# Gate and up projections by seven half-size products, weight sums on VectorE, and an earlier start of each feed-forward

## The chip, the core and the metric

One core of a Trainium2 chip runs the whole program. The metric is the time of one execution on the device in microseconds (us); the median of three runs is given. Engines: TensorE (PE; PEld is its weight load), VectorE (DVE), ScalarE (ACT), GpSimd (POOL) and SyncE (SP), which issues most DMAs.

## What is computed

A block of 2 layers over x (256 tokens by 1024, float32), then a second block of 2 layers. Each first-block layer has an attention and convolution mixer and then a feed-forward: dense in layer 0, a mixture of 8 experts in layer 1. Each second-block layer has a feed-forward, a mixer and a feed-forward. The change concerns the five dense feed-forwards:

```python
def swiglu(x, wg, wu, wd):
    return (jax.nn.silu(x @ wg) * (x @ wu)) @ wd
# first block, layer 0: wg, wu 1024 x 3584, wd 3584 x 1024
x = x + swiglu(rms_norm(x, g), wg, wu, wd)
# second block, four times: wg, wu 1024 x 2816, wd 2816 x 1024
mod = silu(c) @ ada_w[l] + ada_b[l]          # shifts, scales and gates
h = h + 0.5 * g1 * swiglu_2(modulate(rms_norm_2(h, g), sh1, sc1), wg, wu, wd)
```

## The kernel before, in words

Every engine has one hand-written program; semaphores join them. The stages are numbered: 0 mix1, 1 ffn1 (F = 3584), 2 mix1, 3 moe, 4 ffn2, 5 mix2, 6 ffn2, 7 ffn2, 8 mix2, 9 ffn2 (F = 2816 in each ffn2). X holds the residual, two blocks of 128 tokens. Between stages each token block is squared and scaled (`squares` and `scale` on ACT, `norm` on DVE), turned by 8 transposes on PE (`turn`), and copied with the norm's gain into XT, 8 chunks of 128 features by 256 tokens.

**A dense feed-forward.** Its unit is a slice f of 128 hidden features; there are F/128 of them, 28 or 22. For each, PE's `ffn` (from line 1829) makes gate and up: 2 times 8 matmuls with 128x128 weights against 256 tokens, into PSUM bank f % 3. One float32 `mm` (line 1769) is two records in the trace. ACT then takes the sigmoid of gate (line 744), and DVE makes two products (lines 1155 and 1157) that leave the slice of the hidden layer in HT. PE is one slice ahead: after the products of slice f it makes the four `down` matmuls of slice f - 1 (512 columns each, accumulated in banks 4 to 7 over the whole stage).

**The weights' ring.** All weights go through `ring`, four slots of 2 MB, filled by SP in one fixed order. A feed-forward's keys alternate: `gu` j (the gate and up columns of slices 2j and 2j+1: two DMAs of 1 MB) and `dn` j (the down rows of the same two slices: one DMA of 1 MB). The load of the key at place i waits until the key at place i - 4 is given back, so `gu` j + 2 takes the slot of `gu` j, and `dn` j + 1 that of `dn` j - 1. SP's program (line 495) is strictly in order: `dn` j + 1, then `gu` j + 2, then `dn` j + 2:

```python
rg.plan(("gu", st, j), s_gu(st, 2 * j + 2), parts=2)
rg.plan(("dn", st, j), s_dn(st, j + 1) if 2 * j < nf - 4 else s_y(st, 4))
```

`s_gu(st, 2j + 2)` comes when PE has made the gate and up of slice 2j + 1; `s_dn(st, j + 1)` when it has made `down` of slice 2j + 1.

**The conditioning.** `mod` needs 36 pieces of ada_w (2 MB each), loaded by ACT's queue (`ada_load`, line 733), multiplied and summed by DVE (`ada_sum`, lines 1129 and 1132, eight instructions), and turned into MODC (`ada`, `ada_out`) four pieces at a time. These lie in stages 1 (20 pieces), 4 (8) and 6 (8).

**The end.** The last `down` matmuls of each 128 tokens by 512 columns are given to DVE (`s_y`), which adds them to X. For ffn2 this is `residual`, lines 1180 and 1182. `gate_rows` makes the gates' row (16 records on PE, line 1769, `C,MODC`).

Of the kernel before, what the change touches and what calls it, by code (L numbers as in the profile page):

```python
# [15 lines left out]
P = 128  # L16
# [7 lines left out]
F2 = 2816  # L24
# [105 lines left out]
def build(nc, A, out):  # L130
    with ExitStack() as ctx:
# [25 lines left out]
        EG = QT[:, 0:2, :]  # L157
# [65 lines left out]

        ADA_W = ((GS[:, :, :],), (R[:, 2048:4608].rearrange("p (c n) -> p c n", c=5),
# [15 lines left out]
        FG = M2[:, 2048:3072]  # L240
# [46 lines left out]
        s_xta = signal("s_xta", mix1=4, ffn1=4, moe=4, ffn2=4, mix2=4)  # L287
# [5 lines left out]
        s_gu = signal("s_gu", ffn1=28, ffn2=22)  # L293
        s_sig = signal("s_sig", ffn1=28, moe=16, ffn2=22)
        s_silu = signal("s_silu", ffn1=28, moe=16, ffn2=22)
        s_h = signal("s_h", ffn1=28, moe=16, ffn2=22)
# [117 lines left out]
        ADA_SUM, ADA_MM, ADA_OUT = {}, {}, {}  # L414
        for st, first, batches, unit in ((1, 0, 5, lambda b, i: 5 * b + i + 1), (4, 20, 2, lambda b, i: 9 * b + 2 * i + 1),
                                         (6, 28, 2, lambda b, i: 9 * b + 2 * i + 1)):
            for b in range(batches):
                for i in range(4):
                    ADA_SUM[st, unit(b, i)] = first + 4 * b + i
                ADA_MM[st, unit(b, 3) + 1] = first // 4 + b  # L420
                ADA_OUT[st, unit(b, 3) + 2] = first // 4 + b
        ADA_FIRST = {1: 0, 4: 20, 6: 28}
        ADA_LAST = {1: 20, 4: 28, 6: 36}
# [50 lines left out]
        PT1 = np.cumsum([0] + NKC1).tolist()  # L474

# [188 lines left out]
        def _(e):  # L664
# [28 lines left out]
            def squares(st):  # L693

                for b in range(2):
# [3 lines left out]
                    scale(st + 1, b)  # L699

            def turn(st, gain, shift=None):
                base = 4 if st in (1, 3) else 0
# [14 lines left out]
            def gate_rows(st):  # L717

                for h in range(2):
                    e.wait_ge(*s_gbt(st, h + 1))  # L720
                    e.activation(GB[:, h * 512:h * 512 + 512], PS[:, 4 + h, :], ACT.Copy,
# [14 lines left out]
            def ffn(st, F):  # L736
                if st in ADA_LAST:
                    ada_load(ADA_FIRST[st])
                    ada_load(ADA_FIRST[st] + 1)
                for f in range(F // P):  # L740
                    e.wait_ge(*s_gu(st, f + 1))
                    if f >= 2:
                        e.wait_ge(*s_h(st, f - 1))
                    e.activation(EG[:, f % 2, :], PS[:, f % 3, 0:256], ACT.Sigmoid).then_inc(s_sig.sem, 1)  # L744
                    if (st, f) in ADA_SUM and ADA_SUM[st, f] + 2 < ADA_LAST[st]:
                        ada_load(ADA_SUM[st, f] + 2)
                squares(st)
# [128 lines left out]
            def moe(st):  # L876
# [12 lines left out]
                def turned(n):  # L889
# [12 lines left out]
                for n, (ex, f, W) in enumerate(ROUNDS):  # L902
                    if n:
                        turned(n - 1)
# [12 lines left out]
                turned(15)  # L917
# [9 lines left out]
                for b in range(2):  # L927
                    scale(st + 1, b)
# [22 lines left out]
            def mix2(st, l):  # L951
                turn_mod(st, l, 1)
                gate_rows(st)
# [90 lines left out]
            turn(1, lambda c: vcol("ffn_norm_g", 0, c))  # L1044
# [3 lines left out]
            for l in range(2):  # L1048
                st = 4 + 3 * l
                turn_mod(st, l, 0)  # L1050
                gate_rows(st)
                ffn(st, F2)
                mix2(st + 1, l)
                turn_mod(st + 2, l, 2)
                gate_rows(st + 2)
# [4 lines left out]
        def _(e):  # L1060
# [40 lines left out]
            def turn(st, gain, shift=None):  # L1101
                base = 4 if st in (1, 3) else 0
# [1383 lines left out]
```

## Time and profile before

| | us |
|---|---|
| runs shown | 3113.36, 3119.49, 3120.49; median 3119.49 |
| the profiled execution, its own time | 3116.34 |
| its span (first to last instruction) | 3114.5 |
| PE busy | 2968.5 (95% of the span) |
| DVE busy | 823.8 (26%) |
| ACT busy | 395.1 (13%) |
| mean granted TensorE clock | 0.975 |

A row of the profile has line, engine, operation, tiles and shapes, the count, the busy time in us and the mean duration of one in ns. Matmuls are pipelined and the ends that the trace gives them are modelled, so the pace of a stream is read from the starts of two neighbouring groups, not from the mean duration.

### The profile page before, as it was taken

The numbers are of one execution on the slowest core, as the hardware profiler recorded it, in microseconds if no ns is written. First come the engines' busy times: TensorE is split into PE (matmuls) and PEld (weight loads), VectorE is DVE, ScalarE is ACT, GpSimd is POOL, SyncE is SP. The second block draws the span as 40 slices with busy tenths as digits, with TensorE's granted clock in tenths as the row PEclk, the third lists the DMA queues.
The fourth block names the chain that finished last, engine by engine and source line by source line (L and its number), as shares of the span: only waits on it lengthen the run. The fifth ranks groups of instructions, "written<-read, shape, count | busy, mean of one in ns | idle before, by whom it ended". The sixth has DMA issues, their size and how long they took to land.

```text
span 3114.5 us, 34448 instructions
## 1 busy us (share of the span) xinstructions
PE 2968.5 (95%) x15102; PEld 1777.4 (57%) x15102; DVE 823.8 (26%) x1717; ACT 395.1 (13%) x1015; POOL 153.4 (5%) x221
## 2 busy tenths in 40 slices
PE   7699999889999999999997999999999999999998
PEld 5457776543333333333334776586776776576776
DVE  4735453741000000000001333242333002242002
ACT  4420003430000000000001001131001001131000
POOL 6200003300000000000000000000000000000000
PEclk9899999889999999999998999999999999999999
DMA  6149884317999999999996764324764444413442
GB/s 218 68 150 318 286 304 152 116 55 268 377 371 393 358 368 393 358 368 391 359 372 231 260 213 162 122 90 154 257 216 136 149 152 154 140 55 135 149 142 94
DMA packets 266289, 704.58 MB, mean 226 GB/s; under 512 B 9286, under 2 KB 132439, under 8 KB 241556
## 3 DMA queue, kind: packets, MB, share of 16 engines
q1 hardware_dynamic: 225072, 622.39, 54.7%
q10 hardware_dynamic: 38036, 75.61, 6.9%
q0 software_dynamic: 3024, 4.31, 0.5%
q8 instruction: 121, 1.98, 0.3%
q14 instruction: 36, 0.29, 0.0%
HBM read 698.07 MB, written 1.05 MB: 224 GB/s over the span
## 4 chain that ended last, share of the span: by engine, by line
PE 87%; DVE 7%; DMA 3%; ACT 2%; issue 1%; POOL 0%; DVEq 0%; SPq 0%; ACTq 0%
PE PS L1769 84%; DMA ring<-in_moe_w_up_dram 2%; DVE PS L1271 1%; DMA ring<-in_w_in_dram 1%; PE PS L2151 1%; PE PS L1986 0%; DVE SM L1398 0%; DVE SM L1652 0%; DVE GS L1324 0%; ACT R L1004 0%; PE PS L1795 0%; ACT R L685 0%; PE PS L2359 0%; DVE PS L1649 0%; DVE R L1246 0%
## 5 line engine op out<-in xcount | busy, mean ns | idle before, releaser
L1769 PE MATMUL PS<-XT,ring 128*128 128x256 f32 x4480 | 1003.9, 383 | 11.8 <-ACT GS L984 8.0
L1769 PEld LDWEIGHTS PS<-XT,ring 128*128 128x128 f32 x4480 | 857.4, 192 | 178.8 <-issue 56.3
L1769 PE MATMUL PS<-ring,R 128*32 128x256 f32 (+2 forms) x3616 | 718.6, 489 | 0.6 <-ACT R L893 0.6
L1769 PEld LDWEIGHTS PS<-ring,R 128*32 128x32 f32 (+2 forms) x3616 | 291.2, 137 | 367.3 <-issue 330.7
L1769 PE MATMUL PS<-ring,GS 128*64 128x384 f32 (+4 forms) x2176 | 305.2, 527 | 1.0 <-ACT XT L913 0.8
L1769 PE MATMUL PS<-ring,KZ 128*64 128x512 f32 (+3 forms) x2048 | 301.8, 543 | 0.6 <-DMA ring<-in_moe_w_up_dram 0.5
L1155 DVE TENSOR_TENSOR QT<-QT,PS 128x256 f32<-128x256 f32 x116 | 48.9, 421 | 828.3 <-ACT QT L744 828.3
L1769 PEld LDWEIGHTS PS<-ring,GS 128*32 128x32 f32 (+1 forms) x2176 | 103.3, 122 | 197.5 <-issue 192.8
L1769 PEld LDWEIGHTS PS<-ring,KZ 128*64 128x64 f32 (+1 forms) x2048 | 99.7, 123 | 196.8 <-issue 190.8
L1769 PE MATMUL PS<-ring,XT 128*128 128x512 f32 (+2 forms) x512 | 197.9, 548 | 1.2 <-ACT XT L708 1.2
L744 ACT ACTIVATE QT<-PS 128x256 f32<-128x256 f32 x116 | 44.5, 384 | 1092.7 <-PE PS L1769 1092.7
L1769 PEld LDWEIGHTS PS<-ring,XT 128*128 128x128 f32 x512 | 98.1, 192 | 98.9 <-issue 93.7
L1542 DVE TENSOR_TENSOR QT<-QT,PS 128x1536 f32<-128x1536 f32 (+1 forms) x16 | 24.9, 1554 | 439.4 <-PE PS L1769 439.4
L893 ACT ACTIVATE R<-PS 128x512 f32<-128x512 f32 (+1 forms) x32 | 17.4, 544 | 638.2 <-PE PS L2151 638.2
L1132 DVE SCALAR_TENSOR_TENSOR KZ<-GS,CACT,KZ 128x512 f32<-128x512 f32 x126 | 94.7, 752 | 4.5
L1132 DVE SCALAR_TENSOR_TENSOR KZ<-R,CACT,KZ 128x512 f32<-128x512 f32 x126 | 94.7, 752 | 4.5
L626 POOL TENSOR_TENSOR M<-M,GS 128x256 f32<-128x256 f32 x120 | 87.5, 748 | 49.7 <-ACT GS L773 45.5
L1530 DVE TENSOR_TENSOR QT<-QT,PS 128x1536 f32<-128x1536 f32 (+1 forms) x16 | 24.9, 1554 | 179.5 <-ACT QT L908 179.5
L1769 PE MATMUL PS<-ring,MT 128*128 128x512 f32 x128 | 62.4, 638 | 0.0
L650 POOL DMA_DIRECT2D R<-R x16 | 8.4, 527 | 1019.2 <-ACT R L899 1019.2
L1769 PE MATMUL PS<-KZ,QT 128*128 128x256 f32 (+1 forms) x256 | 55.4, 362 | 2.8 <-ACT R L843 2.4
L1769 PE MATMUL PS<-ring,QT 128*128 128x512 f32 x128 | 55.5, 594 | 2.5 <-DVE QT L1739 2.5
(320 smaller groups left out, 1660.3 us busy)
## 6 DMA issues: line engine op xcount, KB each, us to landing
ring<-in_moe_w_gate_dram SPq DMA_DIRECT2D x32, 2048.0 KB, 11.1
ring<-in_moe_w_up_dram SPq DMA_DIRECT2D x32, 2048.0 KB, 10.9
ring<-in_moe_w_down_dram SPq DMA_DIRECT2D x32, 2048.0 KB, 10.9
ring<-in_moe_w_gate_dram SPq DMA_DIRECT2D x32, 1536.0 KB, 11.3
ring<-in_moe_w_up_dram SPq DMA_DIRECT2D x32, 1536.0 KB, 7.1
ring<-in_moe_w_down_dram SPq DMA_DIRECT2D x32, 1536.0 KB, 8.4
ring<-in_ffn_wg_dram SPq DMA_DIRECT2D x44, 1024.0 KB, 5.5
ring<-in_ffn_wu_dram SPq DMA_DIRECT2D x44, 1024.0 KB, 8.0
```

What stands on the lines that cost most here:

```text
L626: e.tensor_tensor(Y[:, ch, :], Y[:, ch, :], CTP[:, m % 8, :], ADD).then_inc(s_cadd.sem, 1)
L650: e.dma_start(YS[0:64, 512 * h:512 * h + 512], YC[64 * h:64 * h + 64, 0:512]).then_inc(s_ys.sem, 16)
L744: e.activation(EG[:, f % 2, :], PS[:, f % 3, 0:256], ACT.Sigmoid).then_inc(s_sig.sem, 1)
L893: e.activation(HM[:, r, 0:W], PS[:, 3 + r, 0:W], ACT.Copy).then_inc(s_hta.sem, 1)
L1132: w = e.scalar_tensor_tensor(out=acc, in0=rows[c], scalar=CACT[:, 1, c:c + 1], in1=acc, op0=MUL, op1=ADD)
L1155: e.tensor_tensor(ev, ev, PS[:, f % 3, 0:256], MUL).then_inc(s_silu.sem, 1)
L1271: t = e.scalar_tensor_tensor(out=y, in0=h, scalar=w, in1=y, op0=MUL, op1=ADD)
L1530: e.tensor_tensor(h, h, PS[:, 0:3, 0:W], MUL).then_inc(s_silu.sem, 1)
L1542: e.tensor_tensor(h, h, PS[:, 3:6, 0:W], MUL).then_inc(s_h.sem, 1)
L1769: return e.matmul(o, lhsT, rhs, start=first, stop=last)
L2151: w = e.transpose(PS[:, 3 + r, c * P:c * P + P], h[:, c, :], ident)
```

## The change

Pairs of slices take the place of slices: the unit is now j, with 256 hidden features, and there are 14 of them in stage 1 and 11 in each ffn2. The multiplication of 256 tokens by 1024 features by 256 hidden features is split into halves in all three directions. For gate and up each, seven products of halves take the place of eight (Winograd's form of Strassen's method). Product m of pair j is 2 times 4 `mm`s with 128x128 weights against 128 tokens, 16 records. Three of the seven use the weights as loaded. The other four use sums of weight blocks, `t_sum(st, j, 1)` to `(st, j, 4)`, each one DVE instruction of 1024 elements per partition; the third overwrites a block of `gu` j in the ring. The token side has four sums (SS) per stage, 512 elements each. ACT copies product 1 out of PSUM (CP). DVE joins the products in seven additions of 256 elements (`join`); the sigmoid and the two products behind it work on 512 elements.

On PE the order in a pair is product 1, 2, 6, 5, 7, 3, 4 and then all eight `down` matmuls of pair j - 1. Product 4 goes to the place of product 1 in PSUM and waits for the join `u2`. `gu` j is given back when product 4 of pair j is made; `dn` j as before. SP's own code is not touched.

At a stage's beginning, products 1 and 2 of pair 0 and product 1 of pair 1, which need the first token block only, stand before the second block's transposes (`turn_block`); the first block's transposes stand inside the stage before, and three weight sums (`ahead`) before DVE's last additions of that stage. `gate_rows` comes after product 2 of pair 1. The 36 pieces of the conditioning lie in stages 1 (12), 4 (8), 6 (8) and 7 (8), one per pair.

The core of the diff:

```diff
+        TS = [[x.rearrange("p (u c n) -> p u c n", u=2, c=4) for x in y]
+              for y in ((M2[:, 1024:2048], M2[:, 2048:3072], QTF[:, 0:1024]),
+                        (MTF[:, 0:1024], MTF[:, 1024:2048], OA[:, :, :].rearrange("p b n -> p (b n)")))]
+        SS = [R[:, i:i + 512].rearrange("p (c n) -> p c n", c=4) for i in (7168, 7680, 4608, 5120)]
+        U2, U3, U4 = (QTF[:, i:i + 256].rearrange("p (u n) -> p u n", u=2) for i in (1024, 1280, 1536))
+        CP = [x.rearrange("p (u n) -> p u n", u=2) for x in (QTF[:, 1792:2048], R[:, 8192:8448])]
...
+        FIRST2 = [(0, 1), (0, 2), (1, 1), (1, 2)]
+        PRODUCTS = FIRST2 + [(j, m) for j in range(14) for m in (1, 2, 6, 5, 7, 3, 4) if (j, m) not in FIRST2]
+        SUMS = ("c11", "u2", "u4", "u3", "c12", "c22", "c21")
...
-        ADA_FIRST = {1: 0, 4: 20, 6: 28}
-        ADA_LAST = {1: 20, 4: 28, 6: 36}
+                ADA_OUT[st, 4 * b + 5] = first // 4 + b
+        ADA_FIRST = {1: 0, 4: 12, 6: 20, 7: 28}
+        ADA_LAST = {1: 12, 4: 20, 6: 28, 7: 36}
...
-                rg.plan(("gu", st, j), s_gu(st, 2 * j + 2), parts=2)
+                rg.plan(("gu", st, j), made(st, j, 4), parts=2)
...
+        def product_bank(j, m):
+
+            if m in (1, 2, 4):
+                return 3 if j == 1 else 0, 256 * (m == 2)
+            return (1, 256 * (m == 5)) if m in (6, 5) else (2, 256 * (m == 3))
+
...
+                def copy(j):
+
+                    e.wait_ge(*made(st, j, 2))
+                    if j >= 2:
+                        e.wait_ge(*joined(st, j - 2, "u2"))
+                    e.activation(CP[j % 2], product_of(j, 1), ACT.Copy).then_inc(s_cp.sem, 1)
+
+                copy(0)
+                turned(st, 1, (0, 1, 4, 5))
+                copy(1)
+                if st > 1:
+                    gate_rows(st, 6)
                 if st in ADA_LAST:
                     ada_load(ADA_FIRST[st])
                     ada_load(ADA_FIRST[st] + 1)
...
+            def t_sum(st, j, n):
+
+                w = rg.view(("gu", st, j), 16, 256).rearrange("p (u c) n -> p u c n", u=2)
+                b11, b12, b21, b22 = (w[:, :, 4 * k:4 * k + 4, P * m:P * m + P] for k in range(2) for m in range(2))
+                t1, t2, t4 = TS[j % 2]
+                if n == 1:
+                    e.wait_ge(*rg.landed["gu", st, j])
+                    if j >= 2:
+                        e.wait_ge(*made(st, j - 2, 4))
+                    e.tensor_tensor(t1, b12, b11, SUB).then_inc(s_ts.sem, 1)
+                elif n == 2:
+                    e.wait_ge(*s_ts(st, 4 * j + 1))
+                    e.tensor_tensor(t2, b22, t1, SUB).then_inc(s_ts.sem, 1)
+                elif n == 3:
+                    e.tensor_tensor(b12, b22, b12, SUB).then_inc(s_ts.sem, 1)
+                else:
+                    e.wait_ge(*s_ts(st, 4 * j + 2))
+                    e.tensor_tensor(t4, b21, t2, SUB).then_inc(s_ts.sem, 1)
+
...
+                for n in (1, 2, 3):
+                    t_sum(st, 0, n)
...
-                for f in range(F // P):
-                    ev = EG[:, f % 2, :]
-                    e.wait_ge(*s_sig(st, f + 1))
-                    e.tensor_tensor(ev, ev, PS[:, f % 3, 0:256], MUL).then_inc(s_silu.sem, 1)
-                    e.wait_ge(*s_silu(st, f + 1))
-                    e.tensor_tensor(HT[:, f % 8, :], ev, PS[:, f % 3, 256:512], MUL).then_inc(s_h.sem, 1)
-                    if (st, f) in ADA_OUT:
...
+                e.tensor_tensor(SS[0], a21, a22, ADD).then_inc(s_ss.sem, 1)
+                e.wait_ge(*s_ss(st, 1))
+                e.tensor_tensor(SS[1], SS[0], a11, SUB).then_inc(s_ss.sem, 1)
+                e.tensor_tensor(SS[2], a11, a21, SUB).then_inc(s_ss.sem, 1)
+                e.wait_ge(*s_ss(st, 2))
+                e.tensor_tensor(SS[3], a12, SS[1], SUB).then_inc(s_ss.sem, 1)
+                t_sum(st, 0, 4)
+                n = F // 256
+                for j in range(n):
+                    if j + 1 < n:
+                        for m in range(1, 5):
+                            t_sum(st, j + 1, m)
+                    def join(r, out, x, y):
+                        e.tensor_tensor(out, x, y, ADD).then_inc(s_cq.sem, 1)
+
+                    e.wait_ge(*s_cp(st, j + 1))
+                    if j:
+                        e.wait_ge(*s_h(st, j))
+                    join("c11", CQ[:, :, 0, :], CP[j % 2], product_of(j, 2))
+                    e.wait_ge(*made(st, j, 5))
+                    join("u2", U2, CP[j % 2], product_of(j, 6))
+                    e.wait_ge(*joined(st, j, "u2"))
+                    join("u4", U4, U2, product_of(j, 5))
+                    e.wait_ge(*made(st, j, 3))
+                    join("u3", U3, U2, product_of(j, 7))
+                    e.wait_ge(*joined(st, j, "u4"))
+                    join("c12", CQ[:, :, 2, :], U4, product_of(j, 3))
+                    e.wait_ge(*joined(st, j, "u3"))
+                    join("c22", CQ[:, :, 3, :], U3, product_of(j, 5))
+                    e.wait_ge(*made(st, j, 4))
+                    join("c21", CQ[:, :, 1, :], U3, product_of(j, 4))
+                    gq, uq = (CQ[:, u, :, :].rearrange("p q n -> p (q n)") for u in range(2))
+                    e.wait_ge(*s_sig(st, j + 1))
+                    e.tensor_tensor(SIG, SIG, gq, MUL).then_inc(s_silu.sem, 1)
+                    e.wait_ge(*s_silu(st, j + 1))
+                    at = 2 * j % 8
+                    e.tensor_tensor(HT[:, at:at + 2, :].rearrange("p c n -> p (c n)"), SIG, uq, MUL).then_inc(s_h.sem, 1)
...
+                def product(j, m):
+                    key = ("gu", st, j)
+                    w = rg.view(key, 16, 256).rearrange("p (u c) n -> p u c n", u=2)
+                    b11, t3, b21, b22 = (w[:, :, 4 * k:4 * k + 4, P * i:P * i + P] for k in range(2) for i in range(2))
+                    t1, t2, t4 = TS[j % 2]
+                    a11, a12, a22 = XT[:, 0:4, 0:P], XT[:, 4:8, 0:P], XT[:, 4:8, P:2 * P]
+                    wt, x = {1: (b11, a11), 2: (b21, a12), 3: (b22, SS[3]), 4: (t4, a22), 5: (t1, SS[0]), 6: (t2, SS[1]),
+                             7: (t3, SS[2])}[m]
+                    B, at = product_bank(j, m)
+                    if m == 1:
+                        e.wait_ge(*rg.landed[key])
+                        if j == 1 and st == 1:
+                            e.wait_ge(*s_x(0, 4))
+                        elif j > 1:
+                            e.wait_ge(*joined(st, j - 1 if j > 2 else 0, "c21"))
+                    elif m == 6:
+                        if j == 0:
+                            e.wait_ge(*s_ss(st, 2))
+                        else:
+                            e.wait_ge(*joined(st, j - 1, "c22"))
+                        e.wait_ge(*s_ts(st, 4 * j + 2))
+                    elif m == 7:
+                        if j == 0:
+                            e.wait_ge(*s_ss(st, 3))
+                        e.wait_ge(*s_ts(st, 4 * j + 3))
+                    elif m == 3:
+                        if j == 0:
+                            e.wait_ge(*s_ss(st, 4))
+                    elif m == 4:
+                        e.wait_ge(*joined(st, j, "u2"))
+                        e.wait_ge(*s_ts(st, 4 * j + 4))
+                    for u in range(2):
+                        for c in range(4):
+                            if j == 0 and u == 0 and m in (1, 2):
+                                e.wait_ge(*s_xta(st, 4 * (m - 1) + c + 1))
+                            w = mm(PS[:, B, at + u * P:at + u * P + P], wt[:, u, c, :], x[:, c, :], c == 0, c == 3)
+                    w.then_inc(s_m.sem, 1)
 
                 def down(f, b, h):
...
+                product(0, 1)
+                product(0, 2)
+                product(1, 1)
+                turn_block(st, 1)
+                product(1, 2)
+                if st > 1:
+                    l, k = mod_of(st)
+                    gate_rows(st, l, 3 * k + 2, 6)()
+                for j in range(n):
+                    for m in (1, 2, 6, 5, 7, 3, 4):
+                        if j > 1 or m not in (1, 2):
+                            product(j, m)
+                    d = j - 1
+                    if 0 <= d < n - 2:
+                        if d == 0:
+                            if st > 1:
+                                e.wait_ge(*s_gbm(st, 2))
+                        e.wait_ge(*rg.landed["dn", st, d])
                         e.wait_ge(*s_h(st, d + 1))
-                        for b in range(2):
-                            for h in range(2):
-                                w = down(d, b, h)
-                        if d % 2:
-                            w.then_inc(s_dn.sem, 1)
-                    if (st, f) in ADA_MM:
-                        ada(ADA_MM[st, f])
-                for b in range(2):
+                        for f in (2 * d, 2 * d + 1):
+                            for b in range(2):
+                                for h in range(2):
...
+                        if b == 1 and h == 0:
+                            turn_block(st + 1, 0)
```

Order on DVE, one pair of stage 1. Before (L1155 and L1157 are the two products of a slice, L1129 and L1132 a piece of the conditioning):

```order
L1155 TENSOR_TENSOR QT<-QT,PS 128x256 [waits s_sig]
L1157 TENSOR_TENSOR R<-QT,PS 128x256 [waits s_silu]
L1129 TENSOR_SCALAR KZ<-R,CACT 128x512 [waits s_ada1]
L1132 SCALAR_TENSOR_TENSOR KZ<-R,CACT,KZ 128x512 [waits s_vector] x7
L1155 TENSOR_TENSOR QT<-QT,PS 128x256 [waits s_sig]
L1157 TENSOR_TENSOR R<-QT,PS 128x256 [waits s_silu]
```

Now (L1213 to L1221 are the four weight sums of pair j + 1, L1291 the joins of pair j, the second of them u2; s_ring0 is the landing of `gu` j + 1, s_m counts products made):

```order
L1213 TENSOR_TENSOR M<-ring 128x1024 [waits s_m,s_ring0]
L1216 TENSOR_TENSOR M<-ring,M 128x1024 [waits s_ts]
L1218 TENSOR_TENSOR ring<-ring 128x2x4x128
L1221 TENSOR_TENSOR QT<-ring,M 128x1024 [waits s_ts]
L1291 TENSOR_TENSOR M<-R,PS 128x2x128 [waits s_h,s_cp]
L1291 TENSOR_TENSOR QT<-R,PS 128x256 [waits s_m]
L1291 TENSOR_TENSOR QT<-QT,PS 128x256 [waits s_cq]
L1291 TENSOR_TENSOR QT<-QT,PS 128x256 [waits s_m]
L1291 TENSOR_TENSOR M<-QT,PS 128x2x128 [waits s_cq] x2
L1291 TENSOR_TENSOR M<-QT,PS 128x2x128 [waits s_m]
L1311 TENSOR_TENSOR KZ<-KZ,M 128x512 [waits s_sig]
L1314 TENSOR_TENSOR R<-KZ,M 128x512 [waits s_silu]
```

The sums of the next pair, with their wait for the ring, stand ahead of all joins of this pair.

Order on PE, one pair of stage 1. Before (128x256 is gate and up of a slice, 128x512 the down products of the slice before):

```order
L1769 MATMUL PS<-XT,ring 128x256 [waits s_h,s_ring2]
L1769 MATMUL PS<-XT,ring 128x256 x15
L1769 MATMUL PS<-ring,R 128x512 [waits s_h]
L1769 MATMUL PS<-ring,R 128x512 x3
L1769 MATMUL PS<-XT,ring 128x256 [waits s_h]
L1769 MATMUL PS<-XT,ring 128x256 x15
L1769 MATMUL PS<-ring,R 128x512 [waits s_h,s_ring3]
L1769 MATMUL PS<-ring,R 128x512 x3
```

Now (products 1 and 2; 6 and 5; 7 and 3; 4; then the down products of pair j - 1; s_cq counts joins, s_ts weight sums):

```order
L1930 MATMUL PS<-XT,ring 128x128 [waits s_cq,s_ring2]
L1930 MATMUL PS<-XT,ring 128x128 x15
L1930 MATMUL PS<-R,MT 128x128 [waits s_ts,s_cq]
L1930 MATMUL PS<-R,MT 128x128 x15
L1930 MATMUL PS<-R,ring 128x128 [waits s_ts]
L1930 MATMUL PS<-R,ring 128x128 x15
L1930 MATMUL PS<-XT,OA 128x128 [waits s_ts,s_cq]
L1930 MATMUL PS<-XT,OA 128x128 x7
L1930 MATMUL PS<-ring,R 128x512 [waits s_h,s_ring1]
L1930 MATMUL PS<-ring,R 128x512 x7
```

Down products, which before stood behind each slice, now stand together behind product 4, and product 4 has a wait for a join.

## Rows read from the trace of the kernel before

**Rows 1.** The page's first part and chain, whole kernel.

```profile
PE 2968.5 (95%) x15102; PEld 1777.4 (57%) x15102; DVE 823.8 (26%) x1717; ACT 395.1 (13%) x1015; POOL 153.4 (5%) x221
...
PE 87%; DVE 7%; DMA 3%; ACT 2%; issue 1%; POOL 0%; DVEq 0%; SPq 0%; ACTq 0%
```

**Rows 2.** Timeline of PE, stage 7: start us, us, engine, line, operation, tiles, count.

```profile
2474.48 7.07 PE L1769 MATMUL PS<-XT,ring 128*128 128x256 f32 x32
2481.39 3.60 PE L1769 MATMUL PS<-ring,R 128*128 128x512 f32 x8
2484.82 7.07 PE L1769 MATMUL PS<-XT,ring 128*128 128x256 f32 x32
...
2495.16 2.10 PE L1769 MATMUL PS<-XT,ring 128*128 128x256 f32 x9
```

**Rows 3.** Timeline of SP's DMA issues, same stretch.

```profile
2474.68 0.37 SPq L495 DMA_DIRECT2D ring<-in_ffn_wd_dram  x1
2481.58 0.37 SPq L495 DMA_DIRECT2D ring<-in_ffn_wg_dram  x1
2481.99 0.58 SPq L495 DMA_DIRECT2D ring<-in_ffn_wu_dram  x1
2495.36 0.37 SPq L495 DMA_DIRECT2D ring<-in_ffn_wd_dram  x1
```

**Rows 4.** Timeline of PE: streams of 128 columns and what follows them, clock 1.00.

```profile
2048.94 1.06 PE L1769 MATMUL PS<-R 128*128 128x128 f32 x8
2049.83 3.62 PE L1769 MATMUL PS<-XT,ring 128*128 128x256 f32 x16
...
2092.61 1.04 PE L2359 MATMUL PS<-C,R 128*128 128x128 f32 x8
2093.49 1.90 PE L1769 MATMUL PS<-R 128*128 128x64 f32 x16
```

**Rows 5.** Groups by line and form, PE's weight loads with 256 columns, whole kernel.

```profile
L1769 PEld LDWEIGHTS PS<-XT,ring 128*128 128x128 f32 x4480 | 857.4, 192 | 178.8 <-issue 56.3 <-ACT GS L984 8.0 <-DMA ring<-in_w_in_dram 1.7
```

**Rows 6.** Groups by line and form, DVE, whole kernel: busy us, mean ns.

```profile
L1132 DVE SCALAR_TENSOR_TENSOR KZ<-GS,CACT,KZ 128x512 f32<-128x512 f32 x126 | 94.7, 752 | 4.5
...
L1155 DVE TENSOR_TENSOR QT<-QT,PS 128x256 f32<-128x256 f32 x116 | 48.9, 421 | 828.3 <-ACT QT L744 828.3
...
L1182 DVE TENSOR_TENSOR X<-X,M 128x512 f32<-128x512 f32 x24 | 16.6, 692 | 0.8
...
L1711 DVE TENSOR_TENSOR M<-M,SM 128x1024 f32<-128x1024 f32 x2 | 2.4, 1224 | 0.1
```

**Rows 7.** DMA issues at 2482 and 2495, then at 302 beside conditioning: KB, us to landing.

```profile
ring<-in_ffn_wg_dram SPq DMA_DIRECT2D x1, 1024.0 KB, 5.4
ring<-in_ffn_wu_dram SPq DMA_DIRECT2D x1, 1024.0 KB, 7.9
...
ring<-in_ffn_wd_dram SPq DMA_DIRECT2D x1, 1024.0 KB, 5.0
...
ring<-in_ffn_w_gate_dram SPq DMA_DIRECT2D x1, 1024.0 KB, 9.3
ring<-in_ffn_w_up_dram SPq DMA_DIRECT2D x1, 1024.0 KB, 12.4
```

**Rows 8.** Windows: PE, PEld, DVE, ACT, POOL busy us (x), PEclk, DMA share, GB/s.

```profile
2162.00:2164.00 2.00, 0.00 (x0) 0.00 (x0) 1.67 (x8) 0.68 (x1) 0.00 (x0) 1.00 0.77 315
...
2166.00:2168.00 2.00, 2.00 (x5) 1.61 (x6) 0.76 (x2) 1.98 (x5) 0.00 (x0) 0.50 0.75 172
2168.00:2169.00 1.00, 1.00 (x5) 0.86 (x4) 0.00 (x0) 0.84 (x1) 0.00 (x0) 0.85 1.04 403
...
2083.00:2089.00 6.00, 6.00 (x26) 5.55 (x25) 0.42 (x1) 0.61 (x2) 0.00 (x0) 0.50 0.00 0
...
2485.00:2489.00 4.00, 4.00 (x20) 3.51 (x20) 0.00 (x0) 0.00 (x0) 0.00 (x0) 1.00 1.09 353
```

**Rows 9.** The chain in time, from stage 6 to stage 7.

```profile
2384.69 12.46 PE PS L1769 x29
...
2402.07 0.45 PE PS L1795 x2
...
2403.77 46.33 PE PS L1769 x182
```

More of the change, by code:

```diff
@@ L739, in ffn @@
                     ada_load(ADA_FIRST[st] + 1)
-                for f in range(F // P):
[L741 to L746, printed above, removed]
+                for j in range(F // 256):
+                    if j >= 2:
+                        copy(j)
+                    k = ADA_SUM.get((st, j - 1))
+                    if k is not None and k + 2 < ADA_LAST[st]:
+                        ada_load(k + 2)
+                    e.wait_ge(*joined(st, j, "c21"))
+                    if j:
+                        e.wait_ge(*s_h(st, j))
+                    e.activation(SIG, CQ[:, 0, :, :].rearrange("p q n -> p (q n)"), ACT.Sigmoid).then_inc(s_sig.sem, 1)
                 squares(st)
@@ L1162, in ffn @@
+                if STAGES[(st + 1) % 10] == "ffn2":
+                    ahead(st + 1)
                 for b in range(2):
@@ L1870, in ffn @@
-                for b in range(2):
-                    for h in range(2):
-                        for f in range(nf - 4, nf):
-                            if b == h == 0:
-                                if f % 2 == 0:
-                                    e.wait_ge(*rg.landed["dn", st, f // 2])
-                                e.wait_ge(*s_h(st, f + 1))
-                            w = down(f, b, h)
-                        w.then_inc(s_y.sem, 1)
+                              f == 0, f == last)
@@ new lines, in ffn @@
+                e.wait_ge(*rg.landed["dn", st, n - 2])
+                e.wait_ge(*s_h(st, n - 1))
+                for f in (last - 3, last - 2):
+                    for h in range(2):
+                        down(f, 0, h)
+                e.wait_ge(*rg.landed["dn", st, n - 1])
+                e.wait_ge(*s_h(st, n))
+                for h in range(2):
+                    down(last - 1, 0, h)
+                    down(last, 0, h).then_inc(s_y.sem, 1)
+                for h in range(2):
+                    for f in range(last - 3, last + 1):
+                        if h == 1 and f == last - 1 and STAGES[(st + 1) % 10] == "ffn2":
+                            turn_block(st + 1, 0)
+                        w = down(f, 1, h)
+                    w.then_inc(s_y.sem, 1)
@@ L2063, in mix1 @@
                     for h in range(2):
-                        out(b, h, range(4))
+                        if st == 0 and b == h == 1:
+                            out(b, h, range(2))
+                            turn_block(1, 0)
+                            out(b, h, range(2, 4))
+                        else:
+                            out(b, h, range(4))
             def moe(st):
```

192 lines of the change are left out of this document (119 added, 73 removed).

## The prediction

> **What bounds the kernel now.** I read the page first: PE is busy for 95% of the span and holds 87% of the chain [rows 1]. So a microsecond taken off PE inside a stage counts in full, and one added to PE's wait counts too. Then I read PE's timeline in a feed-forward without conditioning work [rows 2]. From the start of 32 records of 256 columns to the start of the next group are 2481.39 - 2474.48 = 6.91 us, 216 ns each. Eight records of 512 columns take 2484.82 - 2481.39 = 3.43 us, 429 ns each. A slice is 10.34 us, a pair of slices 20.68, and there is no gap. SP's issues [rows 3] show why the ring costs nothing now: down's 1 MB goes out at 2474.68, gate and up only 6.9 us later, and nobody needs them for most of a pair.
>
> **The products.** A pair now has 7 x 16 = 112 records of 128 columns for 64 of 256. Streams of 128 columns exist already [rows 4]: 8 records take 2049.83 - 2048.94 = 0.89 us, and 2093.49 - 2092.61 = 0.88 us, so 110 to 112 ns each. The risk is the weight load: a record of the old kind carries a load of 192 ns on average [rows 5], which hid behind 216 ns of matmul. But 192 cannot be its least duration, since 8 loads passed in 0.89 us. Bounds are 110 and 192 ns; I take 111, the rate of the rows of just this shape. A product is then 16 x 0.111 = 1.78 us, seven are 12.43 against 64 x 0.216 = 13.82. That saves 1.39 us per pair, and 14 + 4 x 11 = 58 pairs save 81 us, if nothing waits. The down products stay: 16 x 0.429 = 6.86 us.
>
> The Trainium skill (TensorE: Matmul & The Clock Gate, "Back-to-back issue gap") says that pairs of load and matmul of 128 columns keep up about 81 ns where the columns alone would give 56, and this speaks against the change. An estimate by that ratio, 108 x 81/56 = 156 ns, would make seven products 17.5 us, 3.7 more than before. The rows above, of eight records, do not agree with it; no longer stream of this shape stands in the trace.
>
> **DVE's work per pair.** Four weight sums of 1024 elements at 1.224 us [rows 6] are 4.9 us, 5.0 with the gaps between them. Seven joins at about 0.42 and two products of 512 at 0.69 make 4.3 us. A piece of conditioning is 7 x 0.752 plus about 0.48, 5.7 us. Together 15.0 us of a pair of 19: by busy time DVE fits. What counts is the order.
>
> **The new wait, and what stands behind it.** Follow one pair j from the moment S at which PE starts product 1.
> 1. SP issues in order. `dn` j waits for the down products of pair j - 2, and on PE these are the last thing before S. `gu` j + 1 stands behind `dn` j on SP. Its own slot has been free since product 4 of pair j - 1, 6.86 us earlier; before the change that was the later event, now it is the earlier one. So three DMAs of 1 MB go out together at S.
> 2. When does `up` land? Issued as a pair, gate lands after 5.4 and up 7.9 us after its own issue; down alone takes 5.0 [rows 7]. With issue times of 0.4 us each [rows 3] up lands at S + 0.9 + 7.9 = 8.8, if the third megabyte in front costs nothing. At the 353 GB/s of a full stretch [rows 8] 1 MB is 3.0 us, somewhat less for down's longer rows: 11.4. I take 11.0, near the upper end, since the same DMA engines are full in that stretch. Beside a conditioning load of 2 MB, up took 12.4 instead of 7.9 [rows 7], 4.5 more. I take 3.5 more, 14.5, because that load is issued some 4 us after S; bounds 11 and 16.
> 3. DVE's four sums of pair j + 1 wait for this landing and stand ahead of all joins of pair j. `u2` is ready 5.0 + two joins of 0.42 + 0.06, together 5.9 us later: at S + 16.9, or at S + 20.4 with conditioning.
> 4. PE reaches product 4 at S + 6 x 1.78 = 10.7 and waits for `u2`: 6.2 us, or 9.7.
> 5. Then product 4 (1.78) and the down products (6.86), and the next S. Nothing shortens this chain: each link starts from S.
>
> DVE itself is free in time: after product 4 one join, sigmoid, two products and a piece of conditioning take about 2.5 + 5.7 = 8.2 us, which is 1.4 us after the next S, long before the landing.
>
> **The clock.** While PE stands for 2 us the granted clock is still 1.00; after the gap of which that is a part it is 0.50 (1.2 instead of 2.4 GHz) until 2168.15 or so, and in another place for over 6 us [rows 8]. A wait of 6 us will bring it down each time. Work that takes 3 to 6.4 us at half clock loses 1.5 to 3.2 us; I take 2.4 for each stall. The stall then costs 6.2 + 2.4 = 8.6 us, with conditioning 12.1.
>
> **How often.** Pair 0 has its next weights in the ring, the last pair has no next one. Pair 1: its products 1 and 2 are made early, and `gu` 2 goes out alone after product 4 of pair 0, landing 0.5 + 7.9 = 8.4 later; u2 at 14.3 against four products, 7.1: 7.2 + 2.4 = 9.6 us. So 5 x 9.6 = 48; of the 43 others 10 + 3 x 6 = 28 lie beside a conditioning load, 28 x 12.1 = 339, and 15 x 8.6 = 129. Sum 516 us.
>
> **The stage boundaries.** Now 2403.77 - 2397.15 = 6.6 us pass from the last down product to the first product of the next stage, and second-block transposes start at 2402.07 [rows 9]. The same chain of additions, squares, norm and scaling stays for the second token block, but three products, 5.3 us, move into it. Against that gate_rows (16 records, 1.8 us) comes onto PE's path in ffn2, the 1.2 us of copying before the first product is covered, and pair 0 waits 0.8 us for u2 behind DVE's longer list (copies, four token sums, five weight sums). Net -3.9 us for each ffn2 and -5.7 for stage 1, together -21. DVE's three sums ahead of the last additions, 3.7 us, delay the first block's norm; PE has 9 us of down products there, which hide it, and if that cover is gone up to 3 us per boundary come back. The pieces of conditioning are as many as before and hide under PE both times; only their loads matter, counted above.
>
> **Sum.** -81 - 21 + 516 = +414 on the 3116.3 us of the profiled execution: 3530 us. The median of the runs is 3 us above that execution, which I leave inside the range.
>
> **Rivals.**
> *The ring is in time and the change gains.* This ends on the other side. Its mechanism is `u2` at or before S + 10.7, so up landed by S + 4.8. Then only -102 remain: 3014 us. For it: the slot of `gu` j + 1 is free 6.9 us before S, so an issue then would land in time; DVE has room. Against: the order of SP's list, unchanged in the diff, and 1 MB alone takes 5.0 us. It decides where stalls average 102/48 = 2.1 us, that is up landing about 6.9 us after S; above that the kernel is slower. I give it 0.12, for a misread order rather than for fast DMAs.
>
> *The weight loads set the pace.* If each record of 128 columns takes its load's mean of 192 ns, a product is 3.07 us and a pair 7 x 3.07 + 6.86 = 28.4 us, +7.7; 58 pairs give +446, and beside conditioning u2 (20.4) still comes 2 us after six products (18.4), +56, boundaries -20: about 3600 us. For it stands the mean load duration, against it the rows of 110 to 112 ns. 0.05. The ratio of the Trainium skill above (TensorE: Matmul & The Clock Gate) would go the same way; the trace's short streams do not agree with it.
>
> *Gain and stalls cancel*, because up lands around 7 us after S: 3116 us, 0.02.
>
> *The forecast*, stalls in 48 pairs: 0.81.
>
> **Numbers.** The likeliest case gives 3530. Its low end takes 8.8 and 11 us to landing and 1.5 for the clock: 5.5 and 7.7 us per stall, 8.7 for pair 1, -102 + 44 + 83 + 216 = +241, 3357. Its high end takes 11.4 and 16 and 3.2: 9.8, 14.4 and 10.4, -102 + 52 + 147 + 403 = +500, 3616. I widen the low end a little, since links that I added up may overlap: 3330 to 3620. The gaining case lies outside and holds 0.12. A measurement of this kernel tells about 0.3% from no change: faster 0.12, same 0.02, slower 0.86.
>
> **What would show it.** Right: PE idle before product 4 (`XT,QT` and `XT,OA` of 128 columns) of 5 to 10 us in nearly every pair, released by DVE's join; the first weight sum (1024 elements, out of the ring) waiting for the DMA of up; down, gate and up issued within 1 us of each other; a pair of 26 to 32 us; the clock at 0.50 behind each wait. Products 1 to 3 and 5 to 7 at 110 to 112 ns a record. Wrong: pairs of 19 us with PE dense, or products paced at 150 ns and more with no wait before product 4.

## The result, and the profile after

| | before | after |
|---|---|---|
| median of four runs, us | 3118.97 (3113.36 to 3120.49) | 3576.44 (3573.73 to 3584.68) |
| profiled execution, span | 3116.34, 3114.5 | 3573.73, 3571.2 |
| PE busy | 95% | 84% |
| mean granted clock | 0.975 | 0.912 |

The changed kernel takes 1.147 times as long (95% interval 1.145 to 1.150): slower by 457 us, where the prediction had 414.

Page of the changed kernel, the first part and the chain:

```profile
PE 3000.8 (84%) x17886; PEld 1888.7 (53%) x17886; DVE 1236.5 (35%) x2259; ACT 420.6 (12%) x1055; POOL 152.6 (4%) x221
...
PE 63%; DMA 19%; DVE 13%; issue 2%; ACT 1%; SPq 1%; DVEq 0%; POOL 0%; ACTq 0%
```

Against [rows 1] the chain has lost PE and gained DMA and DVE, together 32% for 10%: the last work to end now waits for transfers and for the sums on them. That PE is busy for slightly longer than before (3000.8 against 2968.5 us), with an eighth less work in gate and up, is the clock; more on it below.

PE's waits of the changed kernel (engine, tile and line, releaser: us in total, times, longest), the row of the stall and the one of gate and up's own load:

```profile
PE PS L1930 <- DVE QT L1291: 429.4, 49, 12.6
...
PE PS L1930 <- DMA ring<-in_ffn_wu_dram: 7.5, 1, 7.5
```

One pair of stage 9, without conditioning: PE's timeline, then SP's issues.

```profile
3344.03 3.73 PE L1930 MATMUL PS<-XT,ring 128*128 128x128 f32 x32
3347.60 3.74 PE L1930 MATMUL PS<-R,MT 128*128 128x128 f32 x32
3351.17 3.74 PE L1930 MATMUL PS<-R,ring 128*128 128x128 f32 x32
3360.67 3.71 PE L1930 MATMUL PS<-XT,OA 128*128 128x128 f32 x16 [5.76 <-DVE QT L1291]
3364.22 7.03 PE L1930 MATMUL PS<-ring,R 128*128 128x512 f32 x16
3371.08 1.17 PE L1930 MATMUL PS<-XT,ring 128*128 128x128 f32 x9
```

```profile
3344.22 0.37 SPq L549 DMA_DIRECT2D ring<-in_ffn_wd_dram  x1
3344.64 0.47 SPq L549 DMA_DIRECT2D ring<-in_ffn_wg_dram  x1
3345.15 0.58 SPq L549 DMA_DIRECT2D ring<-in_ffn_wu_dram  x1
3371.28 0.37 SPq L549 DMA_DIRECT2D ring<-in_ffn_wd_dram  x1
```

Six products pass without a gap, 3.57 us for two, so 111.6 ns a record. Then PE stands for 5.76 us before product 4. A pair takes 27.05 us, where it took 20.68 [rows 2]. SP issues three loads within a microsecond of each other at the pair's start; before, gate and up's issue stood 6.9 us behind down's [rows 3] and the ring was never late. The same pair in the chain of waits, in time (start us, us, what):

```profile
3344.22 0.37 SPq L549
...
3345.15 10.03 DMA ring<-in_ffn_wu_dram
...
3355.20 1.24 DVE M L1213
...
3356.46 1.23 DVE M L1216
...
3358.74 1.22 DVE QT L1221
...
3360.29 0.34 DVE QT L1291
...
3360.67 10.59 PE PS L1930 x32
```

Every link of the loop is here: down's issue (released by PE's last down product), the transfer of up, four sums, two joins, product 4 with the down products, and the next issue. PE's first six products, 10.7 us, are not in it; transfer, sums and joins take 16.4 us beside them. Beside conditioning (stage 1) it is the transfer that is longer, 16.73 us:

```profile
278.72 0.37 SPq L549
...
279.64 16.73 DMA ring<-in_ffn_w_up_dram
...
296.40 1.24 DVE M L1213
...
301.87 10.81 PE PS L1930 x32
```

I went through all 43 pairs that are neither a stage's first two nor its last. From down's issue, up lands after 10.8 to 11.0 us in 14 of them, after 12 to 13 in 6, and after 15.2 to 17.8 in 23. From landing to product 4 it is 5.5 us in every one. The longest of these pairs takes 34.2 us.

### The profile page after: what moved, and what is told of

Same layout as the page of the kernel before. It is cut to its first block, busy times and chain, and to the rows that moved or that the text cites. A ratio compares the mean times of both kernels' runs of the same rounds, so it can differ in the third digit from the quotient of the medians.

```text
span 3571.2 us, 40818 instructions
## 1 busy us (share of the span) xinstructions
PE 3000.8 (84%) x17886; PEld 1888.7 (53%) x17886; DVE 1236.5 (35%) x2259; ACT 420.6 (12%) x1055; POOL 152.6 (4%) x221
## 4 chain that ended last, share of the span: by engine, by line
PE 63%; DMA 19%; DVE 13%; issue 2%; ACT 1%; SPq 1%; DVEq 0%; POOL 0%; ACTq 0%
PE PS L1930 61%; DMA ring<-in_ffn_wu_dram 13%; DMA ring<-in_ffn_w_up_dram 5%; DVE PS L1428 1%; SPq L549 1%; DVE M L1213 1%; DVE QT L1221 1%; DVE M L1216 1%; DVE MT L1213 1%; DVE MT L1216 1%; DVE OA L1221 1%; DMA ring<-in_w_in_dram 1%; PE PS L2367 1%; DVE QT L1291 0%; DVE M L1291 0%
## 5 line engine op out<-in xcount | busy, mean ns | idle before, releaser
L1930 PE MATMUL PS<-XT,ring 128*128 128x128 f32 (+1 forms) x2624 | 400.0, 311 | 16.1 <-ACT GS L1070 7.9
L1930 PEld LDWEIGHTS PS<-XT,ring 128*128 128x128 f32 x2624 | 367.5, 195 | 68.0 <-issue 30.4
L1930 PE MATMUL PS<-XT,OA 128*128 128x128 f32 x432 | 99.6, 424 | 248.3 <-DVE QT L1291 248.3
L1930 PE MATMUL PS<-XT,QT 128*128 128x128 f32 x496 | 99.5, 382 | 181.1 <-DVE QT L1291 181.1
L1930 PEld LDWEIGHTS PS<-XT,OA 128*128 128x128 f32 x432 | 92.2, 324 | 253.2 <-DVE QT L1291 253.2
L1930 PE MATMUL PS<-R,ring 128*128 128x128 f32 x1856 | 216.7, 275 | 0.0
L1930 PEld LDWEIGHTS PS<-R,ring 128*128 128x128 f32 x1856 | 211.9, 192 | 0.0
L1930 PEld LDWEIGHTS PS<-XT,QT 128*128 128x128 f32 x496 | 92.4, 287 | 185.9 <-DVE QT L1291 185.4
L1213 DVE TENSOR_TENSOR M<-ring 128x1024 f32<-128x1024 f32 x31 | 38.0, 1225 | 372.2 <-DMA ring<-in_ffn_wu_dram 276.2
L1291 DVE TENSOR_TENSOR M<-QT,PS 128x256 f32<-128x256 f32 x205 | 80.6, 416 | 139.1 <-PE PS L1930 121.0
L1213 DVE TENSOR_TENSOR MT<-ring 128x1024 f32<-128x1024 f32 x27 | 33.1, 1224 | 265.1 <-DMA ring<-in_ffn_wu_dram 198.2
L1930 PE MATMUL PS<-R,M 128*128 128x128 f32 (+1 forms) x1024 | 121.1, 279 | 1.0 <-DVE R L1280 1.0
```

The lines of the kernel that those rows point to most:

```text
L1213: e.tensor_tensor(t1, b12, b11, SUB).then_inc(s_ts.sem, 1)
L1291: e.tensor_tensor(out, x, y, ADD).then_inc(s_cq.sem, 1)
L1930: return e.matmul(o, lhsT, rhs, start=first, stop=last)
```

## The experiments

The kernel before ran beside these on the same chip: 3119.88 us for `e1` to `e4`, 3118.65 for `e5` to `e8`.

**The order of the loads alone.** `e1_gu_first` lets gate and up of the next pair go ahead of this pair's down, in the ring's plan and in SP's list (the plan's part is shown):

```diff
-            for j in range(nf // 2):
-                rg.plan(("gu", st, j), made(st, j, 4), parts=2)
-                rg.plan(("dn", st, j), s_dn(st, j + 1) if 2 * j < nf - 4 else s_y(st, 4))
+            n = nf // 2
+            rg.plan(("gu", st, 0), made(st, 0, 4), parts=2)
+            for j in range(n):
+                if j + 1 < n:
+                    rg.plan(("gu", st, j + 1), made(st, j + 1, 4), parts=2)
+                rg.plan(("dn", st, j), s_dn(st, j + 1) if j < n - 2 else s_y(st, 4))
```

> One edit to the changed kernel: in the ring's order gate and up of pair j + 1 stand ahead of down of pair j, so that their load is issued when product 4 of pair j - 1 is made, 6.9 us before S, and not behind the down products. Theory (SP's order makes the wait): up lands 1.5 us after S, about 6 us beside a conditioning load; u2 is ready before PE reaches product 4 in plain pairs and 1 us late beside conditioning. A plain pair takes 19.3 us, one with conditioning 20 to 21; the whole 3020 to 3060 us, below the kernel before. Rival (the DMA engines are simply too slow for the weights and the conditioning): the waits stay for the most part, over 3400 us. Rival (weight loads set the pace of 128 columns): the waits go, but a product takes 2.5 to 3.1 us and the whole stays over 3250.

Measured: 3032.94 us (3029.50 to 3034.78), 0.972 of before (0.971 to 0.974). SP's issues and PE's timeline, stage 7:

```profile
2395.47 0.37 SPq L552 DMA_DIRECT2D ring<-in_ffn_wg_dram  x1
2395.88 0.58 SPq L552 DMA_DIRECT2D ring<-in_ffn_wu_dram  x1
2402.34 0.37 SPq L552 DMA_DIRECT2D ring<-in_ffn_wd_dram  x1
```

```profile
2382.77 3.73 PE L1939 MATMUL PS<-XT,ring 128*128 128x128 f32 x32
...
2393.49 1.95 PE L1939 MATMUL PS<-XT,QT 128*128 128x128 f32 x16
2395.27 7.03 PE L1939 MATMUL PS<-ring,R 128*128 128x512 f32 x16
2402.14 3.73 PE L1939 MATMUL PS<-XT,ring 128*128 128x128 f32 x32
```

Gate and up go out as PE leaves product 4, 6.9 us before the pair ends, and a pair is 2402.14 - 2382.77 = 19.37 us without a gap. The same transfers, sums and products as in the changed kernel, in another order on one queue, are worth 543 us. Of PE's wait for the joins this is left:

```profile
PE PS L1939 <- DVE QT L1300: 11.2, 11, 1.4
```

**The order of the sums alone.** `e2_sums_late` keeps SP's order and moves DVE's four sums of pair j + 1 behind the joins of pair j and the two DVE products that make its slice of HT (in `ffn` of DVE, for the same `j + 1 < n`):

```diff
-                    if j + 1 < n:
-                        for m in range(1, 5):
-                            t_sum(st, j + 1, m)
                     def join(r, out, x, y):
...
                     e.tensor_tensor(HT[:, at:at + 2, :].rearrange("p c n -> p (c n)"), SIG, uq, MUL).then_inc(s_h.sem, 1)
+                    if j + 1 < n:
+                        for m in range(1, 5):
+                            t_sum(st, j + 1, m)
```

> One edit to the changed kernel: DVE makes the four weight sums of pair j + 1 behind the last product of pair j and no longer ahead of its joins; SP's order stays. Theory (it is DVE's order that passes the late landing on to product 4): up still lands 11 and 17 us after S, but nobody waits for it; the joins run beside the products, PE does not wait before product 4, and the sums are ready some 3 us before product 6 of the next pair. 3020 to 3060 us. Rival (PE is held by the landing itself, by another way): waits of PE move to product 1 or 6 of the next pair, over 3300 us.

Measured: 3067.87 us (3066.84 to 3068.98), 0.984 of before (0.982 to 0.985). The load still goes out late, and costs hardly anything: `u2` no longer stands behind it. So the stall needs both links, the late issue and the sums ahead of the joins; cutting either frees PE. What is left is one new wait, and one that the changed kernel had too (stage 7, below):

```profile
PE PS L1930 <- DVE MT L1216: 25.6, 5, 5.1
...
PE PS L1930 <- DMA ring<-in_ffn_wu_dram: 7.4, 1, 7.4
```

**Both.** `e3_both` has both edits.

> Both edits together. If each takes the whole wait away, they do not add: within 0.5% of the better of the two, 3010 to 3040 us, pairs of 19.3 us throughout. If each leaves a part, the sum is lower than either by that part. The forecast without waits was 3014 us.

Measured: 3055.82 us (3051.12 to 3056.29), 0.979 (0.978 to 0.981). That is 23 us slower than the first edit alone, a miss. The place is the start of each stage: PE's timeline, then DVE's, stage 1.

```profile
220.25 5.97 PE L1939 MATMUL PS<-R,MT 128*128 128x128 f32 x32 [5.11 <-DVE MT L1225]
226.06 3.74 PE L1939 MATMUL PS<-R,ring 128*128 128x128 f32 x32
```

```profile
217.02 0.69 DVE L1320 TENSOR_TENSOR R<-KZ,M 128x512 f32<-128x512 f32 x1
217.63 1.22 DVE L1222 TENSOR_TENSOR MT<-ring 128x1024 f32<-128x1024 f32 x1
218.88 1.23 DVE L1225 TENSOR_TENSOR MT<-ring,MT 128x1024 f32<-128x1024 f32 x1
```

Pair 1 has two products made early and no down products before it, so its product 6 comes right behind product 4 of pair 0. Its sums stood last in DVE's row, behind all joins of pair 0. The wait is 5.1 us, five times, and the 32 records behind it take 226.06 - 220.25 = 5.81 instead of 3.57 us (5.0 to 6.4 in the five stages). The waits of 25.6 us and the 11 us of slower records are 37; the 11 us of waits that `e1_gu_first` still had are gone, and 26 remain for the 23 measured.

**That miss mended.** `e5_pair1_early` is `e3_both` with the sums of pair 1 ahead of the joins of pair 0, those of the later pairs behind:

```diff
+                    if j == 0:
+                        for m in range(1, 5):
+                            t_sum(st, 1, m)
                     def join(r, out, x, y):
...
-                    if j + 1 < n:
+                    if 0 < j < n - 1:
                         for m in range(1, 5):
                             t_sum(st, j + 1, m)
```

> Gate and up loaded ahead of down (as in e1_gu_first), and DVE's four weight sums behind the second product of the pair before (as in e3_both), but those of pair 1 early, ahead of the joins of pair 0. If e3_both lost 23 us to e1_gu_first only because the sums of pair 1 stood behind the joins of pair 0 (TensorE waited 25.6 us for them, 5 times), those waits go, and so do the 11.2 us in 11 pieces that e1_gu_first still waits at product 4: about 3033 - 11 = 3022 us, 0.969 of before. If late sums cost something of their own beyond pair 1, it stays near e3_both's 3056 us.

Measured: 3020.91 us (3018.82 to 3022.55), 0.968 of before (0.967 to 0.970). Both waits are gone, as expected (0.3 us is left at one product 4). This is the fastest version found, 3.2% under the kernel before and 15.5% under the changed one.

**The transfers beside conditioning.** `e6_cond_small` is the changed kernel with 32 of 512 columns of each conditioning load, the first two apart. The conditioning vectors then lack most of their weights; DVE's work on them is as before:

```diff
-                    e.dma_start(part, w[:, c:c + n, :]).then_inc(s_ada[k % 2], 16)
+                    m = 512 if k < 2 else 32
+                    e.dma_start(part[:, :, 0:m], w[:, c:c + n, 0:m]).then_inc(s_ada[k % 2], 16)
```

> The changed kernel, with all conditioning loads but the first two cut from 2 MB to 1/16 of that (32 of 512 columns; the conditioning vectors then don't get their weights), all of DVE's work on them kept. Theory: the loads of the conditioning that run beside those of the feed-forward make up's slice land at S + 15 to 17.8 us instead of S + 11.0, in 30 pairs, and the sums and product 4 come 146 us later in all (the sum over these pairs of product 4's start less S + 16.4): without them all land at S + 11 and the time is about 3576 - 150 = 3426 us. Rival: the loads land late there for another reason (DVE's conditioning work, the ring's order), then no change, 3576 us.

Measured: 3459.60 us (3457.94 to 3461.27), 117 us less than the changed kernel; 150 were expected. ACT's queue (packets, MB, share of the engines) and up's DMA (KB, us to landing) of one pair in stage 1 (pair 4), the changed kernel:

```profile
q10 hardware_dynamic: 1040, 2.10, 17.1%
...
ring<-in_ffn_w_up_dram SPq DMA_DIRECT2D x1, 1024.0 KB, 16.6
```

and the experiment, same pair:

```profile
q10 hardware_dynamic: 1040, 0.13, 2.4%
...
ring<-in_ffn_w_up_dram SPq DMA_DIRECT2D x1, 1024.0 KB, 11.7
```

Queue 10 is ACT's. With its time almost gone, up lands 4.9 us earlier. Over the 43 pairs the mean landing goes from 14.3 to 11.9 us; 43 x 2.4 = 103 of the 117 us. So the conditioning's bytes are the cause of most of it; that landings beside the small loads stay at 11.4 to 13.2 instead of 11.0 is why 150 was too much. The packets of queue 10 are as many as before (1040), only smaller. The Trainium skill (DMA: Bandwidth & Descriptors, "Queues, rings and completion order") says that each DMA engine takes turns between queues packet by packet; the delay of SP's loads while ACT's is under way fits this, and so does a small rest of it with small packets, but no run here shows the turns themselves.

**Is anything hidden in the loop?** `e7_fifth_sum` and `e8_fifth_sum_gu_first` put one more sum ahead of each pair's first, in the changed kernel and in `e1_gu_first`:

```diff
+                    if j:
+                        e.tensor_tensor(t4, b12, b11, SUB).then_inc(*v.up())
+                        e.wait_ge(*v.last())
                     e.tensor_tensor(t1, b12, b11, SUB).then_inc(s_ts.sem, 1)
```

> The changed kernel with one more weight sum of 1.22 us (its result is overwritten), ahead of the first one of every pair but a stage's first: 53 more operations on DVE. Theory: between the landing of up and product 4 nothing is hidden, so each costs its whole length and the hand-over, about 1.3 us: 53 x 1.3 = 69 us, 3645 us. Rival: the transfers alone set the pace and DVE's sums have slack: no change, 3576 us.

> The same additional sum in the kernel that loads gate and up ahead of down (e1_gu_first, 3033 us). Theory: there the slices land 6 us or more before the sums are due, so the sum is hidden save in pair 1 of a stage and where product 4 already waits (11 places): under 15 us more, 3035 to 3048 us. Rival: DVE's row of work itself is what TensorE waits for, and the sum costs its length in every pair: 3033 + 69 = 3102 us.

Measured: 3638.59 us (3638.14 to 3639.05), +62 us, in the first, 1.17 us for each of the 53 sums: all on the path. In the second 3062.83 us (3061.10 to 3066.97), +30 us, twice what I had allowed and half of the rival's 69. PE's wait for the joins went from 11.2 us in 11 places to this:

```profile
PE PS L1942 <- DVE QT L1303: 30.1, 15, 3.0
```

So 18.9 us come as waits, in few places (both product 4s at the start of a stage, 1.51 and 2.07 us in stage 1, are among them); PE's busy time rose by 2900.7 - 2889.0 = 11.7 us with the same instructions, which is the rest. For 38 of the 53 sums no wait shows. DVE has room there, but less than I thought. The clock takes its part in a few places: behind five of the ten waits of 2.1 to 3.0 us product 4 and the down products take 10.2 to 10.4 us instead of 8.8, which is 8 of the 11.7 us; behind the other five nothing is lost.

**The clock alone.** `e4_warm` is the changed kernel with idle matmuls of 128 columns ahead of product 4, whose results product 4 overwrites: 20, or 46 where a conditioning load was expected beside the pair. A handshake keeps DVE's joins behind them.

```diff
                     elif m == 4:
+                        if 1 <= j < F // 256 - 1:
+                            e.wait_ge(*s_cp(st, j + 1))
+                            for _ in range(46 if (st, j - 1) in ADA_SUM and ADA_SUM[st, j - 1] + 2 < ADA_LAST[st] else 20):
+                                d = mm(PS[:, B, at:at + P], b11[:, 0, 0, :], a11[:, 0, :], True, True)
+                            d.then_inc(s_dum.sem, 1)
                         e.wait_ge(*joined(st, j, "u2"))
```

> The changed kernel with idle matmuls in PE's wait before product 4 (20 of 128 columns in plain pairs, 46 beside conditioning, written over a product that is already copied), so that PE is not idle for more than about 2 us. They change no result. Theory (the clock falls because PE stands): the granted clock stays at 1.00, each of the 48 waits loses 1.8 to 2.2 us less, 3576 - 90 = about 3485 us. Rival (the clock falls for another cause, or the loss is none): 3570 to 3590 us. If the idle matmuls run into product 4, somewhat more.

Measured: 3540.63 us (3533.46 to 3543.56), 36 us less than the changed kernel, where the expectation was 3485. Three pieces of the chain in time, stage 9, show two pairs in which the clock held, with one between in which it did not:

```profile
3281.66 8.94 PE PS L1933 x32
...
3310.01 10.59 PE PS L1933 x32
...
3336.94 8.06 PE PS L1933 x30
```

These are product 4 and the down products: 8.94 us warm and 10.59 behind a cold stretch (the last piece is cut by the window after 30 of 32). I measured this stretch, product 4 to the next issue, in 38 pairs of each kernel. It is 10.99 us on average in the changed kernel, 10.3 to 11.9; with idle matmuls it is 8.95 in 28 pairs and 10.6 in the other 10, where up came after their end and PE stood again for 2.0 to 4.2 us (in two of the 28 it stood for 2.1 us and the clock held). Saved are 43 x 1.6 = 69 us. Against that, in 9 pairs the idle matmuls lasted beyond the moment at which `u2` could have been ready, 36 us in all; in five of them by 5.4 to 6.7 us, up having landed early:

```profile
2001.61 10.44 PE L1933 MATMUL PS<-XT,ring 128*128 128x128 f32 x92
2012.99 2.05 PE L1933 MATMUL PS<-XT,QT 128*128 128x128 f32 x16 [0.94 <-DVE QT L1292]
```

69 - 36 = 33 of the measured 36. The idle work was set by which pairs I thought slow; the clock's part is real, its size was judged too high, and the experiment paid part of it back itself.

## Why the prediction was right, and where it was off

**What bounds the kernel, and the record.** Right. 32 records of 128 columns take 3.57 us, 111.6 ns each; I had 111, and the bound of 192 ns is out. The rival in which weight loads set the pace falls: the groups above run dense for 96 records with as many loads. The Trainium skill (TensorE: Matmul & The Clock Gate, "Back-to-back issue gap"), by whose ratio I had estimated 156 ns, is not borne out by this stream either. Measured dense pairs take 19.37 us for 19.3.

**The saving.** 20.68 - 19.37 = 1.31 us a pair, 76 us for 58 pairs; I had 81. `e5_pair1_early` lays this open: 3022.55 in its profiled execution, 94 under the kernel before, so some 18 us lie outside the pairs, for 21 forecast. For stage 9, PE's timeline before (the last pieces of a longer answer):

```profile
2868.25 1.04 PE L1795 MATMUL PS<-C,R 128*128 128x128 f32 x8
...
3090.46 13.90 PE L1769 MATMUL PS<-ring,R 128*128 128x512 f32 x32
```

and in `e5_pair1_early`:

```profile
2785.80 1.04 PE L1978 MATMUL PS<-C,R 128*128 128x128 f32 x8
...
2793.55 5.52 PE L1942 MATMUL PS<-XT,ring 128*128 128x128 f32 x48
...
2995.76 13.90 PE L1942 MATMUL PS<-ring,R 128*128 128x512 f32 x32
```

Before, the stage takes 3090.46 - 2868.25 = 222.2 us from its first transposes to the last down products. In the other it is 2995.76 - 2793.55, plus the 0.9 us of transposes that now lie in the stage ahead, 203.1. Of the difference of 19.1, 11 x 1.31 = 14.4 are pairs, and 4.7 the boundary, for 3.9 forecast.

**Up's landing.** The plain value was right: S + 11.0, by the stretch's rate, and 11.0 measured. Beside conditioning the term was too small. I took 14.5 and gave 16 as the upper bound; 23 pairs lie between 15.2 and 17.8, beyond the bound in many. I had priced the conditioning load by a trace in which it met 2 MB [rows 7]; now it meets three, on a loop that starts again only when they are through. Fewer pairs than the 28 were hit, which gave part of it back.

**The sums and joins.** 5.5 us measured from landing to product 4, 5.9 forecast. `e7_fifth_sum` shows that nothing there is hidden, `e2_sums_late` that their place in DVE's row is one half of the stall.

**The idle time.** Forecast 5 x 7.2 + 28 x 9.7 + 15 x 6.2 = 401 us in 48 stalls, measured 429.4 in 49 and 7.5 in one other. The 43 pairs account for 385 of it, where 365 were forecast: this is the landing beside conditioning (28 pairs stand 10.5 us on average for 9.7, the 15 plain ones 6.0 for 6.2). The rest, 52 for 36, lies at the start of the stages: product 4 of pair 1 waits 6.7 to 9.7 us, 44 in all, and in stage 7 there is what I did not see: product 1 of pair 1 itself waits for the load.

```profile
2714.60 3.79 PE L1930 MATMUL PS<-XT,ring 128*128 128x128 f32 x16 [7.49 <-DMA ring<-in_ffn_wu_dram]
```

**The clock.** Windows of stage 9 (PE, PEld, DVE, ACT, POOL busy us, then granted clock, DMA share, GB/s):

```profile
3357.00:3358.00 1.00, 0.00 (x0) 0.00 (x0) 1.00 (x2) 0.00 (x0) 0.00 (x0) 0.67 0.00 0
3358.00:3364.00 6.00, 3.33 (x15) 3.33 (x16) 4.03 (x8) 0.00 (x0) 0.00 (x0) 0.50 0.00 0
3364.00:3371.00 7.00, 7.00 (x19) 3.26 (x18) 1.80 (x3) 0.63 (x1) 0.00 (x0) 0.99 0.01 4
```

PE stood from 3354.91, and the clock is at 0.50, 1.2 GHz, before product 4 starts. Product 4 runs at half pace, 3364.22 - 3360.67 = 3.55 us for 1.79; the down products are warm again. This plain stall so loses 1.8 us for the 2.4 I took. In total PE is busy for 3000.8 us here and for 2885.3 in `e5_pair1_early`, with the same 17886 matmuls. Those 115.5 us are what 48 x 2.4 gave, but in part by luck. From product 4 to the next issue the 43 pairs take 10.97 us on average, against 2402.34 - 2393.49 = 8.85 in `e1_gu_first` above: 2.1 us each, 91 in all, 2.2 beside conditioning and 2.0 in plain pairs. Pair 1 of the five stages adds 11.5. The other 13 us lie outside these stretches; 1.8 of them are the product behind the load in stage 7, the rest I have not placed. So 2.4 was somewhat too much for one stall.

**The sum.** Against `e5_pair1_early` the span is 551 us longer, 437 idle and 115 slower clock; forecast were 516. The gain came out 8 us smaller than forecast, the idle time 36 larger: 3530 + 44 = 3574, the profiled execution. The pairs beside conditioning were longer than the 32 us that I had named as a sign, up to 34.2, by the same landing. The rivals: the gaining one, 3014 us, is the kernel `e5_pair1_early` (3021), once the order is mended. Its pairs start the load 6.9 us before S, as that rival asked.

## What to carry to other kernels

When two keys share one in-order queue, ask for each which event releases it, and put first the one that is released first and needed first; a change that moves one release later or earlier can turn a harmless order into a loop. Draw that loop once (issue, transfer, the work on it, the consumer, the next release): all of it is paid, however idle each engine is. On an engine that serves both the loop and its consumer, work for the next round goes behind the joins that this round waits for, but not in the first round of a stage, which has less cover.

## What the runs showed that I had not expected

- Three loads of 1 MB behind one another land 11.0 us after the first issue; with 2 MB of another queue under way, up to 17.8. Cutting these 2 MB to 0.13, with as many packets, brought the last load of the example from 16.6 to 11.7 us, counted from its own issue, not to the 10.0 of a plain pair.
- Idle matmuls hold the clock, in 28 of 38 pairs: 8.95 us for product 4 and down against 10.99. They are worth it only where the length of the wait is known; half of their gain went into those that lasted too long.
- The two cures are not additive. Each alone removes nearly all of the stall, and together they were 23 us slower than the better one, for an order at stage starts that one of them brought along.
